# Spreading one head's gate rows over all partitions: a split once, then one rounded product, in a hybrid decoder step

## What is computed

```python
beta = sigmoid(b);  g = -exp(A_log) * softplus(a + dt_bias)          # (B, T, H)
G = cumsum(g, axis=-1)                                                # in chunks
decay = where(incl, exp(where(incl, G[..., :, None] - G[..., None, :], 0)), 0)
kk = einsum('nbhtk,nbhsk->nbhts', k, k)
M = eye(C) + where(strict, beta[..., :, None] * kk * decay, 0)
u = triangular_solve(M, v * beta[..., None])
w = triangular_solve(M, k * (beta * exp(G))[..., None])
Aqk = einsum('nbhtk,nbhsk->nbhts', q, k) * decay
qg = q * exp(G)[..., None];  kd = k * exp(G[..., -1:] - G)[..., None];  gl = exp(G[..., -1])
```

## Time and profile before

| | |
|---|---|
| median of 3 runs | 1766.4 us (1765.22 to 1766.65) |
| the profiled execution, its own time | 1768.08 us |
| its span, first to last instruction | 1766.1 us |
| PE busy | 1671.6 us, 95% |
| PEld busy | 1581.0 us, 90% |
| DVE busy | 1098.8 us, 62% |
| ACT busy | 699.7 us, 40% |
| POOL busy | 55.5 us, 3% |
| memory traffic, mean | 76 GB/s |
| mean granted PE clock | 0.982 of full |
| chain that ended last | PE 77%, DVE 12%, ACT 5%, issue 4% |

### The profile page before, as it was taken

The page is one execution under the profiler, slowest core; times in us unless marked ns, Lnnn a source line. Parts: engine busy times, 40 slices in busy tenths (PEclk is TensorE's granted clock), DMA queues, the critical chain, the costliest instruction groups (busy, mean ns, idle before and its releaser), DMA issues.

```text
span 1766.1 us, 33069 instructions
## 1 busy us (share of the span) xinstructions
PE 1671.6 (95%) x12555; PEld 1581.0 (90%) x12555; DVE 1098.8 (62%) x2160; ACT 699.7 (40%) x1220; POOL 55.5 (3%) x101
## 2 busy tenths in 40 slices
PE   6999999899999999999999999999898999999996
PEld 6988888899999999999887787778788999999996
DVE  6888888866534353557768777777845535343444
ACT  5555555524212221225455545554524212122222
POOL 0000000000000000000011100101110000000000
PEclk9999999999999999999999999999998999999997
DMA  5223222223223223222221222122122333223221
GB/s 173 61 76 85 83 77 81 73 71 94 86 84 96 84 84 94 83 73 73 62 64 38 62 63 58 29 74 63 51 60 70 88 88 92 84 87 91 83 71 50
DMA packets 257848, 135.07 MB, mean 76 GB/s; under 512 B 6746, under 2 KB 256180, under 8 KB 257780
## 3 DMA queue, kind: packets, MB, share of 16 engines
q1 hardware_dynamic: 219920, 113.35, 22.8%
q10 hardware_dynamic: 37860, 20.76, 4.0%
HBM read 122.09 MB, written 12.00 MB: 76 GB/s over the span
## 4 chain that ended last, share of the span: by engine, by line
PE 77%; DVE 12%; ACT 5%; issue 4%; ACTq 1%; DVEq 0%; DMA 0%
PE pj L522 61%; PE rr L560 3%; PE rr L543 2%; DVE w_lo L1624 2%; PE rr L640 1%; DVE pr L1967 1%; PE rr L685 1%; PE rr L678 1%; PE rr L827 1%; PE rr L807 1%; ACT w_hi L1054 1%; DVE ws L2037 1%; PE rr L843 1%; DVE ws L1655 1%; PE rr L754 1%
## 5 line engine op out<-in xcount | busy, mean ns | idle before, releaser
L522 PE MATMUL pj<-xh,w_hi 128*128 128x272 f32 x2064 | 454.5, 301 | 16.4 <-DVE w_lo L1624 12.3
L1054 ACT ACTIVATE w_hi<-w_raw 128x1024 fp32r<-128x1024 f32 x211 | 222.4, 1054 | 568.9 <-PE pj L522 552.4
L522 PE MATMUL pj<-xh,w_lo 128*128 128x272 f32 x2064 | 429.4, 290 | 0.0
L522 PE MATMUL pj<-xl,w_hi 128*128 128x272 f32 x2064 | 428.0, 289 | 0.0
L522 PEld LDWEIGHTS pj<-xh,w_hi 128*128 128x128 f32 x2064 | 324.7, 190 | 39.7 <-issue 19.1
L522 PEld LDWEIGHTS pj<-xl,w_hi 128*128 128x128 f32 x2064 | 326.3, 190 | 0.0
L522 PEld LDWEIGHTS pj<-xh,w_lo 128*128 128x128 f32 x2064 | 325.1, 190 | 0.0
L1624 DVE TENSOR_TENSOR w_lo<-w_raw,w_hi 128x1024 fp32r<-128x1024 f32 x211 | 257.1, 1219 | 34.8 <-ACT w_hi L1054 34.7
L522 PE MATMUL pj<-oh,w_hi 128*128 128x272 f32 x1254 | 266.3, 294 | 12.1 <-DVE w_lo L1624 9.4
L522 PE MATMUL pj<-oh,w_lo 128*128 128x272 f32 x1254 | 262.3, 291 | 0.0
L522 PE MATMUL pj<-ol,w_hi 128*128 128x272 f32 x1254 | 261.4, 290 | 0.0
(11 more groups left out here) (318 smaller groups left out, 1982.7 us busy)
## 6 DMA issues: line engine op xcount, KB each, us to landing
w_raw<-in_mlp_w_up_dram SPq DMA_DIRECT2D x64, 512.0 KB, 4.1
w_raw<-in_mlp_w_down_dram SPq DMA_DIRECT2D x64, 512.0 KB, 3.9
w_raw<-in_hgrn_w_in_dram SPq DMA_DIRECT2D x32, 512.0 KB, 4.1
w_raw<-in_gdn_w_in_dram SPq DMA_DIRECT2D x32, 512.0 KB, 4.1
out_dram<-S ACTq DMA_DIRECT2D x16, 512.0 KB, 3.4
S<-in_state_hgrn_dram ACTq DMA_DIRECT2D x8, 512.0 KB, 4.0
w_raw<-in_hgrn_w_out_dram SPq DMA_DIRECT2D x8, 512.0 KB, 3.9
S<-in_state_gdn_dram ACTq DMA_DIRECT2D x8, 512.0 KB, 4.0
```

The source lines that it names most:

```text
L522: last = mm(pj[:, s, b, 0:HALF], w[:, s, k, :], v[:, k, b * HALF:(b + 1) * HALF], start=(k == 0 and a == 0), stop=(k == end - 1 and a == 2))
L1054: f(w_hi[:, c % SPLIT, 0:n], w_raw[:, slot, 0:n], ACT.Copy).then_inc(w_high, 1)
```

## The change: what it does

After `gt4` is filled, its partitions 0 to 63 are split once: ACT rounds them to fp32r into `gate_parts[0:64]` ("high"), and DVE writes the remainder into `gate_parts[64:128]` ("low"). For a head, DVE now multiplies two indicator columns by the head's selector column, which gives `head_rows`, 128 x 2 ("gsel"). An indicator now has ones in two groups of partitions: 0 to 31 and 64 to 95 for `gb`, 32 to 63 and 96 to 127 for `bb`, so that the product adds rounded part and remainder. PE's products have `head_rows` broadcast as the stationary operand and `gate_parts` moving, both fp32r. `gt4` itself moves to a spare row of the work area `ws`, which is free in that stage.

```diff
-    cf[0:32, C_IND] = 1
-    cf[32:64, C_IND + 1] = 1
+    cf[:, C_IND] = p // 32 % 2 == 0
+    cf[:, C_IND + 1] = p // 32 % 2 == 1
...
-        hc = sb("hc", [P, 16])
+        hc = sb("hc", [P, 6])
...
-        gt4 = sb("gt4", [P, T])
+        gt4 = gd["spare"]
+        gate_parts = sb("gate_parts", [P, T], F32R)
+        head_rows = sb("head_rows", [P, 2], F32R)
...
                     for b in range(2):
-                        last = mm(rr[:, (0 if own else 2) + b, 0:HALF], cf[:, C_IND + g:C_IND + g + 1].broadcast_to([P, P]),
-                                  work[:, b * HALF:(b + 1) * HALF], start=True, stop=True)
+                        last = mm(rr[:, (0 if own else 2) + b, 0:HALF], head_rows[:, g:g + 1].broadcast_to([P, P]),
+                                  gate_parts[:, b * HALF:(b + 1) * HALF], start=True, stop=True)
...
             pe.wait_ge(st["gp"][1].sem, st["gp"][1].after("cols", 0))
+            pe.wait_ge(st["gp"][0].sem, st["gp"][0].after("low", 0))
             gdn_prepare("L3", 0)
...
                 sem_of(v, "turn", 0)
+                sem_of(s, "be", 0)
+                s.did(f(gate_parts[0:64], gt4[0:64], ACT.Copy), "high")
                 s.did(f(gt4[96:96 + H], gt4[0:H], ACT.Exp), "eg")
...
-                    v.did(ts(work, gt4[:], hc[:, 4:5], None, ALU.mult), "gsel")
+                    v.did(tt(head_rows[:], cf[:, C_IND:C_IND + 2], hc[:, 4:5].broadcast_to([P, 2]), ALU.mult), "gsel")
...
                 after(st["gp"][1], "cols", 0)
+                after(st["gp"][1], "high", 0)
+                st["gp"][0].did(tt(gate_parts[64:128], gt4[0:64], gate_parts[0:64].bitcast(F32), ALU.subtract), "low")
                 gdn_prepare("L1first", 0)
```

More of the change, by code:

```diff
@@ L257, in build @@
                 "snew", "pred64", "on", "og", "lo"],
-            gp=["x", "neg", "ls", "g", "g2", "scan", "dl", "turn"],
+            gp=["x", "neg", "ls", "g", "g2", "scan", "dl", "turn", "low"],
             ga=["cols", "gsel", "k1", "k2", "k3", "kneg", "kls", "q1", "q2", "q3", "qneg", "dec", "ks", "qls",
@@ L279, in build @@
             hr=["e2", "e4", "vT", "kdT", "e8", "kdTs", "e16", "e32", "os", "e64", "oo", "sq", "ln", "rn", "hi"],
-            gp=["A", "exp", "ln", "be", "el", "eg", "cols"],
+            gp=["A", "exp", "ln", "be", "el", "high", "eg", "cols"],
             ga=["hist", "past", "ktap", "qtap", "vhist", "kexp", "kln", "G", "ksig", "qexp", "qln", "bb", "dec",
@@ L1584, in _ @@
             nc.vector.memset(epsc[:], EPS).then_inc(unit_out, 2)
-            for buf in (hg["KL"], hg["QL"], hg["A"], gt4[:], gcol[:], dtb[:], xp[:]):
+            for buf in (hg["KL"], hg["QL"], hg["A"], gt4, gcol[:], dtb[:], xp[:]):
                 nc.vector.memset(buf, 0.0)
```

## The result

The changed kernel takes 1774.51 us (median of 5 runs, 1772.92 to 1775.30) against 1766.40 us before (5 runs, 1764.45 to 1766.65). The ratio is 1.0047, with a 95% interval of 1.0036 to 1.0059: about 8.1 us slower. That is past the 0.2% that a measurement of this kernel can tell from no change, on the side that the forecast gave 7%. The profiled execution took 1774.68 us, with a span of 1772.5 and a mean granted clock of 0.975; before it was 1768.08, 1766.1 and 0.982.

A forecast was written before the change was run, and what follows sets the result against it. PE was taken as the bound at head 0, while in the loop it waits for ACT. Head 0's -1.33 us, all other terms 0, took the 1766.4 us median to 1765.1 us, 80% range 1762.6 to 1768.0.

The forecast's parts named there:

- the side that the forecast gave 7%: Whole kernel: a measured time slower than 1769.9 us, given 7%.
- Heads 1 to 7 ... Term: 0: Loop over heads: shorter products only lengthen PE's waits for ACT; 0, up to -0.67 us a place if the releaser is wrong.
- one of 1.08 that I gave: Loop, behind the first gate product: PE's idle time for ACT's L1456 grows from 0.41 to 1.08 us.
- this mechanism as a rival: Loop, at 1063 in each head: about 2.0 us idle brings half clock, 1.7 us a stretch, 1777.0 us in all; 7%.
- Head 0, -1.33 us: Head 0's gate products on the chain: PE reaches the sum over features 1.33 us earlier, and the path follows.
- The added work on ACT and DVE, 0: Ahead of head 0: ACT's rounding (0.66 us) and DVE's 0.30 us more fit into idle time; 0.
- The price of the product: PE's gate products: four fp32r matmuls cost 0.50 us in place of 1.83, at L522's 0.125 us each.
- What would have shown it wrong: Profile after: a shorter loop period, PE waiting for DVE ahead of L736, or clock under 1.00 between 880 and 1310 us.
- Two more signs: Profile after: PE's busy time falls about 10 us; waits at a head's two L845 are 1.1 and 2.0 us, total 3.1.

The follow-up runs named there:

- e3: Changed kernel with bb of the seven loop heads in float32, gb and head 0 in fp32r: 1768.46 us, ratio 1.0009 to before.
- e4: Changed kernel with gb of the seven loop heads in float32, bb and head 0 in fp32r: 1773.16 us, ratio 1.0037 to before.
- e11: Changed kernel, unchanged, profiled a second time: 1772.98 us in one execution.
- e2: Changed kernel with the loop's gate products in float32 and only head 0's in fp32r: 1766.50 us, ratio 1.0005 to before.
- e1: Changed kernel with all gate products in float32 again, its changes on ACT and DVE kept: 1767.08 us, ratio 1.0001 to before.
- e6: Changed kernel with one later projection tile (six matmuls) moved behind x32 and bb: 1762.08 us, ratio 0.9974 to before.
- e9: Kernel before the change, unchanged, profiled a second time: 1767.54 us in one execution.
- e10: Kernel before the change, unchanged, profiled a third time: 1765.31 us in one execution.
- e12: Changed kernel with all gate products in float32 again, profiled a second time: 1767.24 us in one execution.
- e5: Changed kernel with each fp32r gate product of the loop issued four times, head 0's once: 1766.80 us, ratio 1.0001 to before.
- e8: Changed kernel with two projection tiles moved behind x32 and bb: 1762.23 us, ratio 0.9977 to before.
- e13: Changed kernel with head 0's gate products in float32, the loop's in fp32r: 1772.98 us in one execution.
- e14: Changed kernel with head 0's gate products in float32, the loop's in fp32r, second execution: 1771.11 us.

## Why the prediction was wrong

**The failed step is "Heads 1 to 7 ... Term: 0".** Its reasoning on who releases PE held: the idle time behind `bb` grew from 1.35 to 2.01 us. Behind `gb` there are two pieces, 0.36 and 0.46 us, in place of one of 1.08 that I gave: PE now comes to `x16` before ACT has done what it needs, a wait that I had not thought of; it brings no half clock (e3). What I left out of the term is that PE's idle time is not free: without the 0.67 us that the product lost, the clock falls. I had this mechanism as a rival, with its place, and gave it 7%, because the clock was 1.00 over a loop with 31.6 us of idle time. That was an argument from the sum over a loop; what decides is one piece with what lies around it. e3 and e4 both shorten one product a head by 0.67 us, and only in the one that lengthens the piece of 1.35 us to 2.00 does the loop fall to half clock, with a period of 61.30 in place of 60.56 us. The term was 0 and measured 5.2 to 5.6 us: seven times 0.74, and up to 0.4 more in the last piece.

**The size of that rival was too large.** I had 1.7 us a stretch, half of 3.40 us. In the head shown PE took 3.68 us from `dt32` to `x64` before, 0.35 of them waiting, and takes 4.53 after without a wait: the stretch held it up by 1.20 us, not 1.7. It came to `x64` 0.93 us late, and 0.74 are left at the end of the period (0.78 in e11, 61.36 against 60.58); where the other 0.2 us go was not followed. With the 5.6 us of the seven stretches and nothing from head 0, the rival would have come to 1772.0 us. Of the measured difference of the medians, 8.1 us, some 2.5 us stay unplaced; that is the size by which the spans of the kernel before differ among three profiles (2.8 us), but the medians should not hide so much. e4, with the same long piece in the loop and only `gb` of the loop still in float32, is at 1773.16 us against 1766.12, 7.0 us over.

**Head 0, -1.33 us: the step is right, its sum is not.** The product fell from 1.83 to 0.51 us on the chain, the square was not late, and DVE's wait ahead of L2040 is 0.36 us, where 0.38 was forecast and it was 1.71 before. But a half-clock stretch ahead of the loop took it back: 47.78 to 47.91 us in the two profiles, which is -1.33 and +1.46. The prediction had no term for that stretch. e2 shows the short product without the loop's change, and its interval overlaps that of e1: no gain can be told.

**The added work on ACT and DVE, 0: right.** The rounding took 0.66 us and ACT's idle time behind it went from 2.24 to 1.56; "eg" still came in time. The remainder took 0.72 us, the selectors 0.16, and L1758 follows with no idle time left, in place of 0.52. e1, with all this and the old products, is at 1.0001.

**The price of the product: right.** 0.51 us for four, and half of the records.

**What would have shown it wrong** was named, a granted clock under 1.00 between 880 and 1310 us; it is 0.97. Two more signs came out otherwise: PE's busy time was to fall by about 10 us and is 1671.6 us in both profiles, since the slower matmuls fill what the shorter products freed, and the waits at the two L845 of a head are 0.46 + 2.01 = 2.47 us and not 3.1.

## What to carry to other kernels

Before taking work off an engine whose clock follows its activity, look at the idle piece that the work borders on, not at the loop's mean clock: in this kernel a saving that went into idle time brought nothing at best (`gb`, e3), and 0.67 us less of PE's work cost 0.74 us a head. Try to put other work of the same engine into the place, as e6 did; that was worth 0.3% with or without the change. And a rival whose ingredients all stand in the trace (a long idle piece, a half clock after such a piece elsewhere) deserves an estimate for one period, and more than a few per cent.

## What the runs showed of the hardware

In this loop an idle piece of 1.35 us, once in 60.6 us, never brought the half clock (seven heads each of before, e1, e2, e3, e9, e10, e12), nor did the pieces in that place in e5 to e8, all of 1.3 us and less, and one of 2.0 us did so in 34 of 35 heads (after, e4, e11, e13, e14). The lower clock begins 0.1 to 1.6 us after PE goes on, when it is busy again. Ahead of the loop, an idle piece of 1.30 us, of the same length in all kernels, was followed by half clock in nine of sixteen executions. The short product of head 0 some 30 us earlier goes with it in fifteen of them, the place of the piece against the regular row on which the stretches of a trace begin goes with it in all sixteen. Why the piece of 1.30 us there can bring it and the one of 1.35 us in the loop never did stays open. Matmuls that only write the same result again (e5) are enough to keep the clock.
